# One core, two transformer blocks in split fp32: products joined over both halves of the operand in the two feed-forwards, and first groups of the next stage placed between the last residual groups

## What is computed

```python
# first block
proj = rms_norm(x, ln1) @ w_in                 # 2048 -> 11280 columns
y_a  = gated_deltanet(...) @ w_branch_a
y_b  = moba_attention(...) @ w_branch_b
x = x + (sigmoid(gate_a) * y_a + sigmoid(gate_b) * y_b) @ w_out
u = causal_dwconv(rms_norm(x, ln2) @ w_up, ffn_conv, ffn_conv_bias)     # 2048 -> 2*5632
x = x + (silu(u_gate) * u_val) @ w_down
x = rms_norm(x, final_norm)
# second block
z = rms_norm(x, attn_norm_2) @ w_in_2          # pool, r/k/v and low-rank columns
x = x + concat(pool_out, rwkv_out) @ w_out_2
x = x + square(relu(rms_norm(x, mlp_norm_2) @ w_ffn_up_2)) @ w_ffn_down_2   # 2048 -> 8192 -> 2048
x = x + sigmoid(rms_norm(x, ple_norm_2) @ w_ple_gate_2) * (p_2 @ w_ple_proj_2)
out = rms_norm(x, final_norm_2)
```

## Time and profile before

| | us |
|---|---|
| median of 3 runs | 3005.17 (3000.43 to 3006.7) |
| the profiled execution | 2999.01, of which the span on the core 2997.2 |
| PE busy | 2914.5 (97% of the span), 23504 matmuls |
| DVE busy | 1891.2 (63%) |
| ACT busy | 1464.3 (49%) |
| POOL busy | 175.4 (6%) |

### The profile page before, as it was taken

One profiled execution on the slowest core, in us unless ns is written; L12 is line 12 of the kernel. 1 busy time (PEld: TensorE's weight loads), 2 busy tenths in 40 slices (PEclk: granted clock), 3 DMA queues, 4 the chain that ended last, 5 costly groups with the idle time before them and its releaser, 6 DMA issues.

```text
span 2997.2 us, 54743 instructions
## 1 busy us (share of the span) xinstructions
PE 2914.5 (97%) x23504; PEld 2848.6 (95%) x23504; DVE 1891.2 (63%) x2130; ACT 1464.3 (49%) x1891; POOL 175.4 (6%) x143
## 2 busy tenths in 40 slices
PE   8999999999999999999999999999899999999998
PEld 8988899999999999999998998898899999999997
DVE  6467765456566666666667667557655555655565
ACT  5356555444454444444446556554544444444454
POOL 1010110000000000000001012021000000000000
PEclk9999999999999999999999999989999999999999
DMA  6534423555555555555555532313465666566654
GB/s 216 186 117 153 157 90 104 183 184 174 191 176 190 183 177 189 184 183 177 182 186 158 170 92 85 113 50 97 133 183 183 184 183 183 183 181 185 183 175 134
DMA packets 134979, 482.19 MB, mean 161 GB/s; under 512 B 14896, under 2 KB 18352, under 8 KB 134608
## 3 DMA queue, kind: packets, MB, share of 16 engines
q1 hardware_dynamic: 134736, 478.68, 50.5%
HBM read 476.53 MB, written 2.10 MB: 160 GB/s over the span
## 4 chain that ended last, share of the span: by engine, by line
PE 84%; DVE 7%; ACT 4%; issue 3%; DMA 1%; POOL 0%; DVEq 0%; SPq 0%; ACTq 0%; POOLq 0%
PE psm L187 76%; PE psb L187 7%; ACT ar L203 2%; DVE ar L225 2%; DVE ar L215 1%; DVE slo L215 1%; DMA raw<-in_w_in 1%; PE psb L190 1%; ACT shi L203 1%; DVE x L215 1%; DVE gl L225 0%; ACT L203 0%; DVE ar L229 0%; ACT hh L203 0%; ACT gf L203 0%
## 5 line engine op out<-in xcount | busy, mean ns | idle before, releaser
L215 DVE TENSOR_TENSOR slo<-raw,shi 128x1024 fp32r<-128x1024 f32 (+1 forms) x901 | 1128.5, 1258 | 711.6 <-ACT shi L203 710.5
L203 ACT ACTIVATE shi<-raw 128x1024 fp32r<-128x1024 f32 (+1 forms) x901 | 947.6, 1054 | 1157.7 <-PE psm L187 980.7
L187 PE MATMUL psm<-gh,shi 128*128 128x256 f32 x3664 | 1051.8, 287 | 18.9 <-DVE slo L215 15.3
L187 PE MATMUL psm<-gl,shi 128*128 128x256 f32 x3664 | 1040.7, 284 | 0.0
L187 PE MATMUL psm<-gh,slo 128*128 128x256 f32 x3664 | 1040.6, 284 | 0.0
L187 PE MATMUL psm<-hh,shi 128*128 128x256 f32 x3408 | 977.5, 287 | 18.2 <-DVE slo L215 9.7
L187 PE MATMUL psm<-hl,shi 128*128 128x256 f32 x3408 | 967.8, 284 | 0.0
L187 PE MATMUL psm<-hh,slo 128*128 128x256 f32 x3408 | 967.7, 284 | 0.0
L187 PEld LDWEIGHTS psm<-gh,shi 128*128 128x128 f32 x3664 | 706.5, 193 | 26.7 <-DVE slo L215 16.5
L187 PEld LDWEIGHTS psm<-gl,shi 128*128 128x128 f32 x3664 | 706.3, 193 | 1.0 <-issue 0.3
L187 PEld LDWEIGHTS psm<-gh,slo 128*128 128x128 f32 x3664 | 705.7, 193 | 0.3
(11 more groups left out here) (199 smaller groups left out, 1322.2 us busy)
## 6 DMA issues: line engine op xcount, KB each, us to landing
raw<-in_w_in SPq DMA_DIRECT2D x240, 512.0 KB, 3.7
raw<-in_w_up SPq DMA_DIRECT2D x176, 512.0 KB, 4.0
raw<-in_w_ffn_up SPq DMA_DIRECT2D x128, 512.0 KB, 4.1
raw<-in_w_ffn_down SPq DMA_DIRECT2D x128, 512.0 KB, 3.6
raw<-in_w_down SPq DMA_DIRECT2D x88, 512.0 KB, 3.8
raw<-in_w_out SPq DMA_DIRECT2D x64, 512.0 KB, 3.7
raw<-in_w_ple_gate SPq DMA_DIRECT2D x32, 512.0 KB, 3.9
raw<-in_w_branch_b SPq DMA_DIRECT2D x16, 512.0 KB, 3.5
```

The costliest lines, as they stand in the source:

```text
L187: return self.issued(self.eng and self.eng.matmul(out, lhs, rhs, start=start, stop=stop, skip_group_check=True), cost)
L203: return self.issued(self.eng and self.eng.activation(out, in_, fn, scale=scale, **kw), cost)
L215: return self.issued(self.eng and self.eng.tensor_tensor(out, a, b, op), self.cost(out))
```

## The change

The diff does two things.

1. In `up`, `uv` and `fup`, each group of 512 columns is cut into two halves of 256 columns, with a PSUM slot each and tiles of 4 chunks by 256 columns (the same 1024 values per partition). High and low part of the operand are laid side by side (`hs`, `gs`), and `shi` is multiplied with both by one matmul of 512 columns; `slo` by the high part is one of 256 columns, added to the upper 256 of the 512 PSUM columns. So the low sums stand apart from the high ones, and eviction takes three instructions for each half: ACT copies the low sums, DVE adds the high ones, DVE multiplies with `rb`. The convolution gets two input buffers instead of one, and relu too.
2. At the two seams groups are cut and moved: `lora` is begun after `down` (10, 1) with 4 chunks, goes on after `down` (10, 2) with 4 and after `down` (10, 3) with 8. The first half of `fup` 0 is begun between `out2b` (3, 2) and `out2b` (3, 3). An open group keeps its PSUM slot. `open_fup` is planned after most of `fup` 0, and the scaling of `x` (`scale`, 16 DVE instructions) goes into `first`, a step with each tile, instead of `lanes`.

```diff
+    def paired(name, w, col):
+        group(("half",) + name, w, 0, col, 256, 16, kc=4)
+        group(name, w, 0, col + 256, 256, 16, kc=4)
...
                 group(("down", g - 1, f), "w_down", 512 * (g - 1), 512 * f, 512, 4)
-    group(("lora", 0), "w_in_2", 0, 4096, 288, 16)
+                if g == 11 and f in (1, 2):
+                    lora(4 * f - 4, 4 * f)
+    lora(8, 16)
...
-            group(("out2b", h, f), "w_out_2", 1024 + 256 * h, 512 * f, 512, 2)
+            out2b(h, f)
+            if h == 3 and f == 2:
+                begun(0, 0, 8)
+    begun(0, 8, 12)
+    begun(1, 0, 8)
+    begun(0, 12, 16)
+    begun(1, 8, 16)
...
+        hs = sb("hs", [128, 16, 2, T], FR)
+        gs = sb("gs", [128, 16, 2, T], FR)
+        hh, hl, gh, gl = hs[:, :, 0, :], hs[:, :, 1, :], gs[:, :, 0, :], gs[:, :, 1, :]
...
+                            elif n == 256:
+                                both = (hs if kind_of(name) in ("up", "uv") else gs)[:, o + k, :, :].rearrange("p w t -> p (w t)")
+                                for f in range(2):
+                                    to, c = psum(name)[:, 512 * f:512 * f + 512], slice(128 * f, 128 * f + 128)
+                                    pe.mm(to, sh[:, q, c], both, first, False)
+                                    mm = pe.mm(to[:, 256:512], sl[:, q, c], ah, False, last)
...
+            def evict_low(name, buf, gone):
+                dst = buf[:, 0:2, :] if name[0] == "half" else buf[:, 2:4, :]
+                ps = psum(name).rearrange("p (f w t) -> p f w t", f=2, w=2)
+                if gone:
+                    a.wait_ge(*gone)
+                a.wait_ge(tile_done, end[name])
+                a.act(dst, ps[:, :, 1, :], ACT.Copy).then_inc(act_step, ("low", name))
...
+            def evict_pair(name, buf):
...
+                v.wait_ge(tile_done, end[name])
+                v.wait_ge(act_step, ("low", name))
+                v.tt(dst, ps[:, :, 0, :], dst, ALU.add).then_inc(dve_step, ("evict", name))
+                v.tt(dst, dst, bc(rb, 2), ALU.mult).then_inc(dve_step, ("scaled", name))
...
-                    lanes[2] += [drive("lora"), drive("scale")]
+                    lanes[2] += [scale_when_known(), drive("lora")]
...
+            def scale_when_known():
+                yield [(dve_step, ("rb", 2))]
+                first.append(drive("scale"))
...
+            group(("half", "fup", 0))
+            group(("fup", 0))
+            group(("half", "fup", 0))
             norm_split(3)
             advance("open_fup")
+            group(("fup", 0))
```

More of the change, by code:

```diff
@@ L377, in weight_plan, with group, begun, lora @@
     plan = []
-    def group(name, w, row, col, ncols, nk, kc=2):
-        plan.append((name, [(w, row + 128 * k, kc, col, ncols) for k in range(0, nk, kc)]))
+    def group(name, w, row, col, ncols, nk, kc=2, part=None):
+        first, last = part or (0, nk)
+        plan.append((name, [(w, row + 128 * k, kc, col, ncols) for k in range(first, last, kc)], first, last == nk))
+    def paired(name, w, col):
+        group(("half",) + name, w, 0, col, 256, 16, kc=4)
+        group(name, w, 0, col + 256, 256, 16, kc=4)
+    def begun(half, first, last):
+        group(("half", "fup", 0) if half == 0 else ("fup", 0), "w_ffn_up_2", 0, 256 * half, 256, 16, kc=4, part=(first, last))
+    def lora(first, last):
+        group(("lora", 0), "w_in_2", 0, 4096, 288, 16, part=(first, last))
+    def out2b(h, f):
+        group(("out2b", h, f), "w_out_2", 1024 + 256 * h, 512 * f, 512, 2)
     for g in range(6):
@@ L494, in build @@
         plan, starts = weight_plan(), tile_starts()
-        tiles, end, place = [], {}, {}
-        for i, (name, ts_) in enumerate(plan):
+        tiles, end, slot, before, owner, free = [], {}, {}, {}, [None, None], [0, 1]
+        for name, ts_, _, ends in plan:
             tiles += ts_
-            end[name], place[name] = len(tiles) - 1, i
+            if name not in slot:
+                i = slot[name] = free.pop(0)
+                before[name], owner[i] = owner[i], name
+            if ends:
+                end[name] = len(tiles) - 1
+                free.append(slot[name])
         NT = len(tiles)
         def psum(name):
-            return psm[:, place[name] % 2, :]
+            return psm[:, slot[name], :]
         def evicted(name):
@@ L2136, in vector_program @@
             progs |= {("epi", ("branch_a", g)): merge_a(g) for g in range(4)}
-            progs |= {("epi", n): add_x(n) for n in place if n[0] in ("out", "down", "out2a", "out2b", "fdn")}
+            progs |= {("epi", n): add_x(n) for n in end if n[0] in ("out", "down", "out2a", "out2b", "fdn")}
             progs |= {("epi", (n, g)): conv_up((n, g)) for n in ("up", "uv") for g in range(11)}
@@ L2454, in epilogue @@
                     until((dve_step, "rbn"))
-                elif kind in norm_of and kind != "lora":
-                    while not known((dve_step, ("rb", norm_of[kind]))):
+                elif kind_of(name) in norm_of and kind != "lora":
+                    while not known((dve_step, ("rb", norm_of[kind_of(name)]))):
                         if first:
@@ L2479, in epilogue @@
                         lanes[2].append(drive(("finish", n)))
+            def scale_when_known():
+                yield [(dve_step, ("rb", 2))]
+                first.append(drive("scale"))
             def group(name):
-                i, j = place[name], end[name] - len(plan[place[name]][1])
-                for ti, (_, _, kc, _, n) in enumerate(plan[i][1]):
-                    j += 1
+                got, ts, k, ends = parts.pop(0)
+                assert got == name, (got, name)
+                part = operand(name)[3]
+                for ti, (_, _, kc, _, n) in enumerate(ts):
+                    j = placed[0]
+                    placed[0] += 1
                     at = lo_done.time(j)
-                    if ti == 0 and i >= 2:
-                        freed = evicted(plan[i - 2][0])
+                    if k == 0 and before[name]:
+                        freed = evicted(before[name])
                         until(freed)
                         at = max(at, freed[0].time(freed[1]))
+                    k += kc
+                    while part and not known((dve_step, part(k - 1))):
+                        first_step()
                     ready(at)
@@ L2594, in plan_order @@
                         group(("down", g - 1, f))
+                        if g == 11 and f in (1, 2):
+                            group(("lora", 0))
             norm_split(2)
```

114 lines of the change are left out of this document (73 added, 41 removed).

## The result

The changed kernel takes 2986.39 us (median of 4 executions, 2985.46 to 2992.36), the kernel before 3002.80 us on the same chip (4 executions, 3000.14 to 3006.70). The ratio is 0.995, with an interval of 0.9937 to 0.9963: some 16 us, or 0.5%, faster, where 46.4 us had been forecast. The time lies 10 us above the forecast range. The profiled execution took 2985.60 us with a span of 2983.8, so the two profiles differ by 13.4 us and can be compared stage by stage.

What follows compares the result with a forecast made beforehand. The prediction took PE's own pace to bound the feed-forwards; 32.4 (joining) + 11 (`lora`) + 3 (`fup`) = 46.4 us off the median of 3002.8 gave 2956.4 us, range 2946 to 2976.

Steps and rivals of the forecast that it cites:

- What bounds the kernel: Both feed-forwards: only PE's own pace counts; PE's other idle time lies outside, at the two seams the diff touches.
- Part 1, 32.4 us: Feed-forward rounds: joining turns 2432 triples of 360.0 ns into pairs of 346.7 ns, 13.3 ns each; bounds nothing and 32.4 us.
- Price of the evictions, nothing: Rounds: 59 us more DVE and 45 us more ACT work stay off the path; bounds nothing and 104 us.
- The low point of the lead: Converted weights behind `uv`: least lead over PE, 2.3 us, falls by about 1 us and no pause follows.
- The second `down` or `fdn` group: Takes the PSUM slot of `uv` or `fup` 5.8 us after their end; eviction needs 3.6 us, so 2.2 us to spare.
- The seam at `lora`, 11 us: Moving `lora` pieces between `down` groups and spreading the scaling wins 11 of 13.8 us; bounds -2 and 13.8.
- spread over eight tiles: Scaling of `x` before `rkv`: one DVE run of 8.30 us becomes 1.04 us before each `slo`, ending a 3.19 us pause.
- `down` 2 and 3 in one PSUM slot: At `lora`: each waits for the eviction before it, with 4.2 us of `lora` as cover; even, 0 to 1 us.
- The seam at `fup`, 3 us: Moving half of `fup` 0 and `open_fup` wins 3 us of 4.4 us of pauses; bounds -2 and 4.4.
- The seams give next to nothing: Rival at both seams: DVE and ACT nearly full, two groups share a slot; 2970.4 to 2972.8 us, chance 0.18.
- Pauses in the rounds: Rival: late addition behind `uv` and `fup`, or lead used up, 1 us in each of 27 rounds; 2983 us, chance 0.12.
- slower: Rival: evictions come onto the path, up to 2.73 us exposed 38 times; 3060 us at the worst, chance 0.04.

Runs made afterwards that it cites:

- `pace_nudge`: `join_only` with one more matmul of 64 columns, overwritten at once, ahead of each half group; 2994.53 us.
- `pace_order`: `join_only` with a chunk's two matmuls of 512 columns run first, then its two of 256; 2977.61 us, ratio 0.9928.
- `after_less_act`: Changed kernel without 15 of 16 columns of the norms' squares and their additions, in three of four chunk groups at both seams; 2973.16 us (one execution).
- `after_spread`: Changed kernel with the 16 scaling instructions in a list of their own, two with each weight tile; 2982.34 us (one execution).
- `join_only`: Kernel before with the joined products in both feed-forwards but no moved groups; 2989.55 us, ratio 0.9963.
- `after_pt`: Changed kernel with the small input's load started earlier in `fup` 0 and its split planned two rounds later; 2985.64 us (one execution).
- `seams_only`: Kernel before with `lora` and `fup` 0 cut and moved, only `fup` 0 joined, whole groups of three matmuls elsewhere; 3003.05 us, ratio 1.0011.
- `best`: Changed kernel with matmuls ordered 512, 512, 256, 256, the scaling spread, and the small input's load and split parted; 2966.59 us, ratio 0.9881.

## Why the prediction was wrong, step by step

- **What bounds the kernel.** Right for the rounds: PE is the only limit there, 715.00 busy of 715 us. Right also that the rest of what the diff could win lay in the pauses of the earlier trace rows.
- **Part 1, 32.4 us.** That the joining saves fixed time on PE was right, the size was off: the term measured 3.5 + 7.7 + 6.0 = 17.2 us, plus some tenths for `fup` 0 that the seam hides. The step that failed is "I take 32.4, because both sizes show the same fixed part". Each size alone does; in alternation the pair takes 353.3 instead of 346.7 ns in most of the stretch. The prediction had noted that no row showed a 512-column matmul followed by one of 256, had set the lower bound at nothing for it, and then gave that bound a chance of 0.04 and nothing in between a case of its own. `pace_nudge` shows that the forecast pair exists, in 26 of 76 half groups, and `pace_order` that grouped sizes take 348.3 ns, 11.7 of the 13.3 ns saved. The Trainium skill's 2.5 ns ("TensorE: Matmul & The Clock Gate", section "Wait — 56ns, not 53.3ns?") would make the pair an estimated 357.5 ns; the measured 353.3 in alternation saves 6.7 ns, neither of the two figures that the prediction weighed, and the measurement decides.
- **Price of the evictions, nothing.** Right. DVE is busy 523.96 of 715 us, 73% against 75 forecast. The low point of the lead was to fall by about 1 us. In the first feed-forward it didn't: these rows of DVE and PE are its place in a late round of the changed kernel.

```profile
1485.27 2.30 DVE L215 TENSOR_TENSOR slo<-raw,shi 128x1024 fp32r<-128x1024 f32 x1
1493.05 0.40 PE L187 MATMUL psm<-hs,shi 128*128 128x512 f32 x1
```

  The tile converted at 1487.57 is the last of the `down` tiles, which starts 2.88 us before the up group of 1493.05, at 1490.17: a lead of 2.6 us. Counted like that for every tile, the least of each round is 2.5 to 2.6 us, where before it was 1.7 (the prediction had read 2.3). In the second feed-forward it fell from 4.4 to 3.3 us, by the 1 us forecast. No round came near nothing.

- **The second `down` or `fdn` group**, "It fits, with 2.2 us to spare": right, no row in the rounds names `ar` or `x`.
- **The seam at `lora`, 11 us.** Wrong; it gained 0.75 us to `rkv` (0, 0) and lost 2.3 behind, and its own sign of being wrong, waits for `x` or `slo` in `lora` and `fup` 0, is there. Two steps failed. First, "The work itself stays [...] I leave 1 to 4 us of pauses": DVE's 25 us were 32.1, ACT's 30 were 31.3, and PE had 39 and not 34 us of its own, since the norm's sum on PE falls into the stage. Even so there was room by the sum, and 6.5 us of pauses came, against 6.1 before. That DVE and ACT feed each other in turn and are needed in bursts is the likely reason, with POOL's hold on `slo`, but neither is shown by itself; `after_less_act` shows 8.4 us of the stage hanging on the three together, 6.7 of them at a like clock. The pauses named in the prediction were symptoms, and moving PE's groups moved them to `gf` and `x`. Second, the scaling "spread over eight tiles": it wasn't. The prediction read `first.append` and not that an epilogue empties `first`; `after_spread` shows 5.9 us for that step, more than the 3.19 us named: 4.5 us of pause, and the rest in slow matmuls behind it.
- **`down` 2 and 3 in one PSUM slot, "even, 0 to 1 us".** Nearly right: PE waited 1.38 us there for the addition at 1587.73.
- **The seam at `fup`, 3 us.** Wrong in sign. Half a `fup` group did cover the old 1.49 us pause, for the slot of `out2b` (3, 2), but the plan left out the next wait of the same kind: the second half of `fup` 0 wants the slot of `out2b` (3, 3) one quarter of a group behind its end, and waits 3.76 us. The load that "meets a lead of 6" met DVE's queue: the lead covers `slo`, but the addition of the first half stood behind the split, and its slot was wanted (1.94 us). The largest part wasn't in the prediction at all: the joining itself costs 5.3 us here (67.24 to 72.56 in `join_only`), of which 4.0 us are pauses. A half group ends after 11 us and not 23, and the plan puts the norm's last steps ahead of its eviction, where PE now waits for them:

```profile
2121.55 0.50 PE L187 MATMUL psm<-gs,shi 128*128 128x512 f32 x1 [1.48 <-DVE x L215]
2132.84 0.50 PE L187 MATMUL psm<-gs,shi 128*128 128x512 f32 x1 [2.54 <-DVE slo L215]
2139.92 3.78 PE L187 MATMUL psb<-ar,con 128*128 128x256 f32 x8 [4.04 <-DVE ar L215]
```

  This is the timeline of `join_only`. Moving the first half of `fup` wins 3.5 us of it back (69.09), about the 3 us forecast, but against another starting point. Each part alone costs 5.3 and 3.8 us here, and both together 1.9; with the 1.56 us of the faster pace of `up` 0 that is most of why the parts do better together than their sum.
- **The rivals.** "The seams give next to nothing" (0.18) was right, and no case held a joining that gives half. Those two together make 3002.8 - 17.2 = 2985.6, beside the measured 2986.4. The range ended at 2976 since it crossed neither rival with the other. "Pauses in the rounds" and "slower" did not come about.
- **Sum.** Of 46.4 us forecast, 15.2 us went in PE's pace and 14 in the seams' gains that never came, and the seams took 3.4 us more; 13.4 us are left in the profiled executions with 1 us less in the start and 1.3 more in the middle: 17.2 - 3.4 - 1.3 + 1.0 = 13.5.

## What to carry to other kernels

A duration read from a run of equal instructions prices only such a run; where a change makes sizes alternate, half of the gain can be lost, so try the sizes grouped. A pause that names an engine's tile says who came last, not what is short: before moving work of the waiting engine, add up what the engines that feed it must do in that stretch, and read the planner's lists to the end for where a moved step is really issued. A gain in one part is a new start for the next, as the half groups of part 1 were for the norm at `fup`.

## What the runs showed of the hardware

- A matmul of 512 columns and one of 256 in turn, each with new weights, take 353.3 ns in most stretches and 346.7 in some; the pace holds for tens of us. One matmul of 64 columns ahead of a run of 32 pairs can switch it (26 of 76 runs fast in `pace_nudge`). Two of 512 followed by two of 256 take 348.3 ns for each pair, in all rounds. Why is open.
- A `slo` on DVE, 1024 columns from SBUF to SBUF, takes 1.44 us at most with no long POOL instruction beside it and up to 3.4 us beside one (31 of 59 over 1.5 us in the changed kernel, 30 of 47 before).
- Pauses of 6.5 us in all, the longest of 2.5, in the stage at `lora` went with a granted clock of 0.96 in the changed kernel (47.35 us) and of 1.00 in `after_pt`, `seams_only` and `best` (45.65 to 45.67 us). So pauses of this size may or may not bring slow matmuls, and the difference is 1.7 us. The prediction had counted such matmuls, 4.5 us, as sure to go with the pauses, and none for those that it left.
